# Ffn gate and up: the high and low activation halves in one 512-column product

## The chip, the cores and the metric

The program runs on one core of one Trainium2 chip. Its time is the device time of that core in microseconds. The kernel before took 2307.03 us in the median of three runs (2304.10 to 2308.41). TensorE does the products, ScalarE, VectorE and GpSimd the rest, and SyncE issues nearly all transfers.

## The reference, cut to what matters

Twelve sublayers run one after the other on 256 tokens of width 1024: six mixers (two RWKV, one stick-breaking attention, one sparse attention, two with three kinds of heads) and six feed-forward layers. Only the feed-forward layers are touched. Four of them are of this form, with a SwiGLU of hidden width 2816:

```python
def rms_norm(x, g):
    xf = x.astype(jnp.float32)
    y = xf * lax.rsqrt(jnp.mean(xf * xf, axis=-1, keepdims=True) + RMS_EPS)
    return (y * g.astype(jnp.float32)).astype(x.dtype)

def swiglu(h, w_gu, w_down):
    g, u = jnp.split(h @ w_gu, 2, axis=-1)
    return (jax.nn.silu(g) * u) @ w_down

x = x + swiglu(rms_norm(x, norm_ffn[i]), ffn_w_gu[i], ffn_w_down[i])
```

The other two (layer indices 4 and 5) put a convolution over three neighbouring tokens on the gate, and use GELU:

```python
g, u = jnp.split(h @ w_gu, 2, axis=-1)
g = depthwise_conv_centred(g, cw, cb)
return x + (jax.nn.gelu(g, approximate=False) * u) @ w_dn
```

## The kernel before, in words

Activations lie transposed: 128 channels on the partitions, 256 tokens (S) along the free dimension, eight such tiles (KT) for the width of 1024. Every large product is done in a split form. An operand is cut into a high half, rounded to the type fp32r, and a low half, the rest. Three products of 128x256 are then summed in PSUM: high weight by high activation, high weight by low activation, low weight by high activation (lines 2184 to 2186). A *unit* is one weight block of 1024 by 128 with its 3 x 8 = 24 products; a gate or an up tile of 128 hidden channels is one unit.

SyncE loads the weight blocks into a ring of four (`ring_a`, 512 KB each), and the down blocks into a ring of two (`ring_d`). For each block ScalarE writes the high half (`hi`, line 2269) and VectorE the low half (`lo`, line 2372) into `w_split`, also a ring of four. Semaphores order it all: `w_hi` and `w_lo` count finished halves, `a_used` counts finished units, `dn_hi` and `dn_lo` are the same for the down blocks, and `d_used` counts finished down steps.

A feed-forward layer has 22 tiles of hidden channels, handled in pairs i = 0 to 10 with q = 0 and 1 in a pair. For tile (i, q) TensorE runs `gate_up(i, q)`, two units into the two halves of one bank, B[4+q]. When both are done, VectorE multiplies the bank by the inverse root of the mean square (line 2442), ScalarE applies SiLU (line 2336; GELU on 2339 after the three convolution operations on 2451 to 2456), VectorE multiplies gate by up (2460), ScalarE copies the high half of the result (2342) and VectorE the low half (2464). Only then may `down(i, q)` run: 24 products with the down block into banks 0 to 3, where they are summed over all 22 tiles. TensorE's order is written by hand: `gate_up(i, 0)`, `down(i-1, 1)`, `gate_up(i, 1)`, `down(i, 0)`, so a tile's `down` comes one down step and one gate_up after its own gate_up. The first `down` of a layer has only `gate_up(0, 1)` in front of it. The last two tiles are summed together in `last_two`, after `down(9, 1)`.

Each engine runs its instructions in order. The order on ScalarE and VectorE is that of `tile_pair` in their `ffn`: the splits of two later weight blocks, the split of the down block, then the activation steps of the tile. After the last tile VectorE makes the low halves of the next layer's first blocks, adds banks 0 to 3 to the residual `xT`, and makes the next layer's `h_split`. The inverse root (`root`) is computed on ScalarE once per layer, from sums that TensorE makes (`norm`) behind its first two units.

## Time and profile before

| | |
|---|---|
| median of three runs | 2307.03 us |
| span of the profiled execution, first to last instruction | 2303.6 us |
| granted TensorE clock, mean over the span | 0.988 |
| TensorE busy with products | 2176.2 us (94%) |
| VectorE busy | 1552.0 us (67%) |
| ScalarE busy | 1204.9 us (52%) |
| moved from and to HBM | 141 GB/s over the span |

For the profiled execution only its span is given; the times of the three runs are 0.5 to 4.8 us above it. A matmul's shown duration (283 ns) is longer than its spacing, because matmuls overlap in the pipeline: the pace is read from the starts of successive rows. In the rows, PE is a product, PEld the load of its weights, DVE is VectorE and ACT is ScalarE.

### The profile page before, as it was taken

How to read it: one execution, taken by the hardware profiler on the slowest of the kernel's cores; microseconds unless marked ns; L12 is line 12 of the kernel's file. 1: busy time of each engine (PE TensorE's matmuls, PEld its weight loads, DVE VectorE, ACT ScalarE, POOL GpSimd, SP SyncE). 2: the span in 40 equal slices, each digit the busy share in tenths (PEclk: the TensorE clock that was granted, in tenths of full speed). 3: DMA queues.
4: the chain of work that ended last, by engine and by line, in shares of the span. 5: the costliest groups of instructions: out<-in, count | busy, mean ns of one | idle time of the engine just before them, and what ended most of it. 6: DMA issues, size and time to landing. Idle time of an engine off the chain costs nothing. (4 is left out here: it accounts for less than half of the span.)

```text
span 2303.6 us, 55968 instructions
## 1 busy us (share of the span) xinstructions
PE 2176.2 (94%) x23136; PEld 2079.3 (90%) x23136; DVE 1552.0 (67%) x2405; ACT 1204.9 (52%) x2058; POOL 36.1 (2%) x51
## 2 busy tenths in 40 slices
PE   6887899999999999999989888999999999999998
PEld 6777799999999988899988778999998999898998
DVE  7763465566665688665588735655777777876776
ACT  5733454455544456554458435544676444776443
POOL 0000000000000011000000000000100000100000
PEclk9899999999999999999989999999999999999999
DMA  5310355543455433355533103555333554434553
GB/s 204 128 48 4 110 176 181 180 140 120 153 194 183 163 112 124 123 192 191 183 101 123 54 4 111 192 191 182 129 115 133 193 190 155 147 120 147 182 191 110
DMA packets 88436, 327.16 MB, mean 142 GB/s; under 512 B 9808, under 2 KB 9936, under 8 KB 87632
## 3 DMA queue, kind: packets, MB, share of 16 engines
q1 hardware_dynamic: 87984, 322.66, 41.3%
q8 instruction: 129, 2.11, 0.4%
q0 software_dynamic: 288, 2.10, 0.3%
q14 instruction: 35, 0.29, 0.0%
HBM read 323.67 MB, written 1.05 MB: 141 GB/s over the span
## 5 line engine op out<-in xcount | busy, mean ns | idle before, releaser
L2184 PE MATMUL bank<-h_split,w_split 128*128 128x256 f32 x3176 | 912.7, 287 | 14.3 <-DVE h_split L2403 8.6
L2185 PE MATMUL bank<-h_split,w_split 128*128 128x256 f32 x3176 | 898.1, 283 | 0.0
L2186 PE MATMUL bank<-h_split,w_split 128*128 128x256 f32 x3176 | 897.6, 283 | 0.0
L2372 DVE TENSOR_TENSOR w_split<-ring_a,w_split 128x1024 fp32r<-128x1024 f32 x474 | 568.0, 1224 | 196.9 <-ACT w_split L2269 195.4
L2184 PEld LDWEIGHTS bank<-h_split,w_split 128*128 128x128 f32 x3176 | 602.9, 190 | 26.3 <-DVE h_split L2403 11.3
L2185 PEld LDWEIGHTS bank<-h_split,w_split 128*128 128x128 f32 x3176 | 598.6, 188 | 1.4
L2186 PEld LDWEIGHTS bank<-h_split,w_split 128*128 128x128 f32 x3176 | 597.8, 188 | 0.0
L2269 ACT ACTIVATE w_split<-ring_a 128x1024 fp32r<-128x1024 f32 x474 | 483.4, 1049 | 44.1 <-PE bank L664 23.7
L2206 PE MATMUL bank<-act_split,d_split 128*128 128x256 f32 x1008 | 285.4, 283 | 3.8 <-DVE act_last L2464 2.4
L2207 PE MATMUL bank<-act_split,d_split 128*128 128x256 f32 x1008 | 285.2, 283 | 0.0
L2208 PE MATMUL bank<-act_split,d_split 128*128 128x256 f32 x1008 | 285.1, 283 | 0.0
L2336 ACT ACTIVATE work<-work 128x256 f32<-128x256 f32 x88 | 36.9, 420 | 347.9 <-DVE work L2442 347.9
L2206 PEld LDWEIGHTS bank<-act_split,d_split 128*128 128x128 f32 x1008 | 193.1, 192 | 4.6 <-DVE act_last L2464 2.8
L2208 PEld LDWEIGHTS bank<-act_split,d_split 128*128 128x128 f32 x1008 | 193.2, 192 | 0.0
L2442 DVE TENSOR_TENSOR work<-bank,work 128x512 f32<-128x512 f32 x132 | 90.8, 688 | 151.8 <-PE bank L2186 151.8
L2207 PEld LDWEIGHTS bank<-act_split,d_split 128*128 128x128 f32 x1008 | 192.9, 191 | 0.0
L2439 DVE TENSOR_TENSOR d_split<-ring_d,d_split 128x1024 fp32r<-128x1024 f32 x126 | 153.5, 1218 | 2.5 <-ACT d_split L2333 2.5
L2333 ACT ACTIVATE d_split<-ring_d 128x1024 fp32r<-128x1024 f32 x126 | 131.5, 1043 | 0.0
L2339 ACT ACTIVATE work<-work 128x256 f32<-128x256 f32 x44 | 18.4, 418 | 179.6 <-DVE work L2456 179.6
L2460 DVE TENSOR_TENSOR work<-work 128x256 f32<-128x256 f32 x132 | 56.2, 426 | 64.0 <-ACT work L2336 42.7
L2464 DVE TENSOR_TENSOR act_split<-work,act_split 128x256 fp32r<-128x256 f32 x126 | 53.6, 426 | 61.0 <-ACT act_split L2342 61.0
L2342 ACT ACTIVATE act_split<-work 128x256 fp32r<-128x256 f32 x126 | 52.6, 418 | 61.9 <-DVE work L2460 61.9
(302 smaller groups left out, 3256.4 us busy)
## 6 DMA issues: line engine op xcount, KB each, us to landing
ring_a<-wa SPq DMA_DIRECT2D x474, 512.0 KB, 3.7
ring_d<-wd SPq DMA_DIRECT2D x132, 512.0 KB, 4.3
tab_sb<-tab SPq DMA_DIRECT2D x1, 2384.0 KB, 13.2
hT<-na POOLq DMA_DIRECT2D x2, 1024.0 KB, 5.1
xT<-x SPq DMA_DIRECT2D x1, 1024.0 KB, 4.8
out<-xT SPq DMA_DIRECT2D x1, 1024.0 KB, 3.9
vec_sb<-vec SPq DMA_DIRECT2D x1, 288.0 KB, 4.8
tab_sb<-tab SPq DMA_DIRECT2D x1, 65.0 KB, 4.6
```

The lines of the kernel that those rows point to most:

```text
L2184: mm(dst, w[:, 0, ks], x[:, 0, k, :], start=(k == 0), stop=False)
L2185: mm(dst, w[:, 0, ks], x[:, 1, k, :], start=False, stop=False)
L2186: last = mm(dst, w[:, 1, ks], x[:, 0, k, :], start=False, stop=(k == KT - 1))
L2206: mm(o, w[:, 0, ms], x[:, 0, :], start=(first and m % 2 == 0), stop=False, skip_group_check=True)
L2207: mm(o, w[:, 0, ms], x[:, 1, :], start=False, stop=False, skip_group_check=True)
L2208: return mm(o, w[:, 1, ms], x[:, 0, :], start=False, stop=final, skip_group_check=True)
L2269: A(w_split[:, u % 4, 0, :], ring_a[:, u % 4, :], ACT.Copy).then_inc(s["w_hi"], 1)
L2333: A(d_split[:, q, 0, :], ring_d[:, q, :], ACT.Copy).then_inc(s["dn_hi"], 1)
L2372: v.tensor_tensor(w_split[:, u % 4, 1, :], ring_a[:, u % 4, :], w_split[:, u % 4, 0, :].bitcast(f32), ALU.subtract).then_inc(s["w_lo"], 1)
L2439: v.tensor_tensor(dd[:, 1, :], ring_d[:, q, :], dd[:, 0, :].bitcast(f32), ALU.subtract).then_inc(s["dn_lo"], 1)
L2442: v.tensor_tensor(work[:, 2 * q:2 * q + 2, :], B[4 + q][:, :].rearrange("p (a b) -> p a b", a=2), inv_rms().unsqueeze(1).broadcast_to([P, ...
L2460: v.tensor_tensor(work[:, 2 * q + 1, :], work[:, 2 * q, :], work[:, 2 * q + 1, :], ALU.mult)\
```

## The change

The two products that share the high weight become one. `h_split[:, :, k, :]` holds high and low activation halves, 256 columns each. `wide_unit` multiplies both at once by the high weight, a 128x512 product that fills a whole bank, and then adds the low weight by the high activation into the first 256 columns. A unit has 16 products in place of 24, on the same number of columns: 8 x 512 + 8 x 256 = 24 x 256. Each unit now needs a bank of its own, so tile (i, q) uses banks 4+2q and 5+2q.

The second 256 columns of each bank (the *tail*) have to be added. `gu_half(q, 1)` is the pair of tails of gate and up. ScalarE copies it to `hT` (semaphore `gu_low`), VectorE adds it to the pair of first halves into `work`, waits for its own result, and then multiplies by the inverse root, now from SBUF to SBUF.

The order on ScalarE and VectorE changes too. The splits of the weight blocks for the next pair stand between the activation steps, and the split of the down block stands last in the tile (in the last tile ahead of the last activation step). `last_two` runs the products of the last but one tile for the first four output blocks before it waits for the last tile's activation. SyncE issues a down block ahead of two weight blocks for each tile.

On VectorE, in the first tile of the first feed-forward layer, the program before has these rows (`d_split` is the down block's low half):

```order
L2372 TENSOR_TENSOR w_split<-ring_a,w_split 128x1024 [waits w_hi] x2
L2439 TENSOR_TENSOR d_split<-ring_d,d_split 128x1024 [waits dn_hi,std_ready]
L2442 TENSOR_TENSOR work<-bank,work 128x512 [waits a_used]
L2460 TENSOR_TENSOR work<-work 128x256 [waits silu_ready]
L2464 TENSOR_TENSOR act_split<-work,act_split 128x256 [waits act_hi]
```

And the changed program, at the same place:

```order
L2418 TENSOR_TENSOR w_split<-ring_a,w_split 128x1024 [waits w_hi] x2
L2485 TENSOR_TENSOR work<-bank,hT 128x512 [waits gu_low]
L2489 TENSOR_TENSOR work<-work 128x512 [waits dve_step,std_ready]
L2418 TENSOR_TENSOR w_split<-ring_a,w_split 128x1024 [waits w_hi]
L2508 TENSOR_TENSOR work<-work 128x256 [waits silu_ready]
L2418 TENSOR_TENSOR w_split<-ring_a,w_split 128x1024 [waits w_hi]
L2516 TENSOR_TENSOR act_split<-work,act_split 128x256 [waits act_hi]
L2478 TENSOR_TENSOR d_split<-ring_d,d_split 128x1024 [waits dn_hi]
```

Two weight splits and the down block's split now stand between the product's end and the last row that the first `down` waits for; the down block's split went from the front of the tile to its end.

On VectorE, in the last two tiles of the same layer, before:

```order
L2439 TENSOR_TENSOR d_split<-ring_d,d_split 128x1024 [waits dn_hi]
L2442 TENSOR_TENSOR work<-bank,work 128x512 [waits a_used]
L2460 TENSOR_TENSOR work<-work 128x256 [waits silu_ready]
L2464 TENSOR_TENSOR act_split<-work,act_split 128x256 [waits act_hi]
L2439 TENSOR_TENSOR d_last<-ring_d,d_last 128x1024 [waits dn_hi]
L2442 TENSOR_TENSOR work<-bank,work 128x512 [waits a_used]
L2460 TENSOR_TENSOR work<-work 128x256 [waits silu_ready]
L2464 TENSOR_TENSOR act_last<-work,act_last 128x256 [waits act_hi]
```

And the changed program, at the same place:

```order
L2485 TENSOR_TENSOR work<-bank,hT 128x512 [waits gu_low]
L2489 TENSOR_TENSOR work<-work 128x512 [waits dve_step]
L2508 TENSOR_TENSOR work<-work 128x256 [waits silu_ready]
L2516 TENSOR_TENSOR act_split<-work,act_split 128x256 [waits act_hi]
L2478 TENSOR_TENSOR d_split<-ring_d,d_split 128x1024 [waits dn_hi]
L2485 TENSOR_TENSOR work<-bank,hT 128x512 [waits gu_low]
L2489 TENSOR_TENSOR work<-work 128x512 [waits dve_step]
L2508 TENSOR_TENSOR work<-work 128x256 [waits silu_ready]
L2478 TENSOR_TENSOR d_last<-ring_d,d_last 128x1024 [waits dn_hi]
L2516 TENSOR_TENSOR act_last<-work,act_last 128x256 [waits act_hi]
```

The split of the last down block (`d_last`) stood ahead of the last tile's steps and now stands inside them. The diff:

```diff
-B = [ctx.enter_context(nc.psum_tensor(f"bank{i}", [P, 512], f32)) for i in range(8)]
+banks = ctx.enter_context(nc.psum_tensor("bank", [P, 8, 512], f32))
+B = [banks[:, i, :] for i in range(8)]
+def gu_half(q, a):
+    return banks[:, 4 + 2 * q:6 + 2 * q, a * S:(a + 1) * S]
+def gu_tail(q):
+    return hT[:, 2 * q:2 * q + 2, :]
...
@@ -2120,22 +2129,33 @@
+            def load_down(j, i=0):
+                if L["d"] + j >= 2 or not isinstance(i, int):
+                    sp.wait_ge(s["dn_lo"], i * 2 + (L["d"] + j - 1))
+                sp.dma_start(ring_d[:, j % 2, :], wd[i * 2 + (L["d"] + j), :, :])\
+                    .then_inc(d_loaded[j % 2], 16)
+            def next_tiles(i):
+                for q in range(2):
+                    load_down(2 + q, i)
+                    load(L, 8 + 2 * q, i)
+                    load(L, 9 + 2 * q, i)
...
+            for q in range(2):
+                load_down(q)
+                load(L, 4 + 2 * q)
+                load(L, 5 + 2 * q)
+            with sp.Fori(0, FT // 2 - 2) as i:
+                next_tiles(i)
+            for q in range(2):
+                load_down(FT - 2 + q)
...
@@ -2186,6 +2206,18 @@
+    def wide_unit(L, n, i, bank, x, ready=None):
+        pe.wait_ge(s["w_lo"], i * 4 + (L["us"] + n + 1))
+        w = w_split[:, (L["u"] + n) % 4, :, :]
+        for k in range(KT):
+            if ready:
+                pe.wait_ge(s[ready[0]], ready[1] + k + 1)
+            ks = slice(k * P, (k + 1) * P)
+            mm(bank, w[:, 0, ks], x[:, :, k, :], start=(k == 0), stop=False)
+            last = mm(bank[:, 0:S], w[:, 1, ks], x[:, 0, k, :], start=False, stop=(k == KT - 1))
+        last.then_inc(s["a_used"], 1)
...
@@ -2196,8 +2228,8 @@
-                unit(L, 2 * q + g, i, B[4 + q][:, g * S:(g + 1) * S], h_split,
-                     ready=("h_ready", 8 * L["hs"]) if first and g == 0 else None)
+                wide_unit(L, 2 * q + g, i, B[4 + 2 * q + g], h_split,
+                          ready=("h_ready", 8 * L["hs"]) if first and g == 0 else None)
...
@@ -2217,16 +2249,20 @@
+            pe.wait_ge(s["act_ready"], FT * f + FT - 1)
+            pe.wait_ge(s["dn_lo"], d + FT)
+            for m in range(4):
+                block_of(m, d_split[:, 0, :, :], act_split[:, 0, :, :])
             pe.wait_ge(s["act_ready"], FT * f + FT)
-            pe.wait_ge(s["dn_lo"], d + FT)
-            for m in range(KT):
-                a = block_of(m, d_split[:, 0, :, :], act_split[:, 0, :, :])
-                b = block_of(m, d_last, act_last, final=True)
-                if m == KT - 1:
-                    a.then_inc(s["d_used"], 1)
-                    b.then_inc(s["d_used"], 1)
-                elif m % 2:
-                    b.then_inc(s["down_done"], 1)
+            for b in range(4):
+                for m in (2 * b, 2 * b + 1):
+                    last = block_of(m, d_last, act_last, final=True)
+                last.then_inc(s["down_done" if b < 3 else "d_used"], 1)
+                if b < 2:
+                    for m in (2 * b + 4, 2 * b + 5):
+                        last = block_of(m, d_split[:, 0, :, :], act_split[:, 0, :, :])
+                    if b == 1:
+                        last.then_inc(s["d_used"], 1)
...
@@ -2315,35 +2351,45 @@
+                act.wait_ge(s["a_used"], i * 4 + (u + 2 * q + 2))
+                A(gu_tail(q), gu_half(q, 1), ACT.Copy).then_inc(s["gu_low"], 1)
+                if first and q == 0:
                     root(L)
+                if not final:
+                    hi(L, 2 * q + 4, i)
...
                     A(work[:, 2 * q, :], work[:, 2 * q, :], ACT.Silu).then_inc(s["silu_ready"], 1)
...
+                if not final:
+                    hi(L, 2 * q + 5, i)
+                if final and q:
+                    down_high(q, i, final)
...
                 A(a_[:, 0, :], work[:, 2 * q + 1, :], ACT.Copy).then_inc(s["act_hi"], 1)
+                if not (final and q):
+                    down_high(q, i, final)
...
@@ -2426,21 +2472,21 @@
+                dve.wait_ge(s["gu_low"], i * 2 + (FT * f + q + 1))
+                gu = work[:, 2 * q:2 * q + 2, :]
+                step.did(v.tensor_tensor(gu, gu_half(q, 0), gu_tail(q), ALU.add))
+                if first and q == 0:
                     rms_inverse(L)
-                dd = d_last if final and q else d_split[:, q, :, :]
-                dve.wait_ge(s["a_used"], i * 4 + (u + 2 * q + 2))
-                v.tensor_tensor(work[:, 2 * q:2 * q + 2, :], B[4 + q][:, :].rearrange("p (a b) -> p a b", a=2),
-                                inv_rms().unsqueeze(1).broadcast_to([P, 2, S]), ALU.mult)\
+                step.settle()
+                v.tensor_tensor(gu, gu, inv_rms().unsqueeze(1).broadcast_to([P, 2, S]), ALU.mult)\
                     .then_inc(s["gu_ready"], 1)
...
+                if not final:
+                    lo(L, 2 * q + 4, i)
...
                 v.tensor_tensor(work[:, 2 * q + 1, :], work[:, 2 * q, :], work[:, 2 * q + 1, :], ALU.mult)\
...
+                if not final:
+                    lo(L, 2 * q + 5, i)
+                if final and q:
+                    down_low(q, i, final)
...
                 v.tensor_tensor(a_[:, 1, :], work[:, 2 * q + 1, :], a_[:, 0, :].bitcast(f32), ALU.subtract)\
...
+                if not (final and q):
+                    down_low(q, i, final)
```

## Rows read from the trace of the kernel before

**Rows 1.** The page's busy time: engine, us (share of the span), instructions.

```profile
PE 2176.2 (94%) x23136; PEld 2079.3 (90%) x23136; DVE 1552.0 (67%) x2405; ACT 1204.9 (52%) x2058; POOL 36.1 (2%) x51
```

**Rows 2.** Busy time by stretch, inside a SiLU and a convolution layer: all engines.

```profile
300.00:460.00 160.00, 160.00 (x1337) 160.00 (x1336) 96.41 (x116) 71.20 (x97) 0.00 (x0) 1.00 0.55 188
1790.00:1940.00 150.00, 150.00 (x1254) 150.00 (x1253) 113.41 (x160) 65.31 (x88) 0.00 (x0) 1.00 0.55 186
```

**Rows 3.** Timeline of PE at half the granted clock: start us, us, engine, line.

```profile
1183.18 0.41 PE L2186 MATMUL bank<-h_split,w_split 128*128 128x256 f32 x1
1183.39 0.41 PE L2184 MATMUL bank<-h_split,w_split 128*128 128x256 f32 x1
```

**Rows 4.** Timeline of PE behind a layer's first two units, plain fp32 products.

```profile
295.76 1.02 PE L2175 MATMUL bank<-sq,tab_sb 128*128 128x256 f32 x4
```

**Rows 5.** Groups by line and shape: count, busy us, mean ns, idle before.

```profile
L2442 DVE TENSOR_TENSOR work<-bank,work 128x512 f32<-128x512 f32 x132 | 90.8, 688 | 151.8 <-PE bank L2186 151.8
L2413 DVE TENSOR_TENSOR sq<-sq 128x512 f32<-128x512 f32 x30 | 20.8, 692 | 6.4 <-ACT sq L2309 4.3
L911 ACT ACTIVATE planes<-bank 128x512 f32<-128x512 f32 x44 | 24.5, 594 | 82.8 <-PE bank L546 53.9 <-PE bank L502 27.5 <-PE bank L558 1.3
```

**Rows 6.** Timeline of ACT at the start of the first feed-forward layer.

```profile
295.13 2.00 ACT L2269 ACTIVATE w_split<-ring_a 128x1024 fp32r<-128x1024 f32 x2
297.04 0.45 ACT L2277 ACTIVATE work<-bank,tab_sb 128x256 f32<-128x256 f32 x1
297.53 0.42 ACT L2279 ACTIVATE work<-work 128x256 f32<-128x256 f32 x1
297.85 1.05 ACT L2333 ACTIVATE d_split<-ring_d 128x1024 fp32r<-128x1024 f32 x1
298.92 1.28 ACT L2336 ACT_TABLE_LOAD   x1
```

**Rows 7.** Timeline of DVE there.

```profile
296.22 2.36 DVE L2372 TENSOR_TENSOR w_split<-ring_a,w_split 128x1024 fp32r<-128x1024 f32 x2 [1.13 <-ACT w_split L2269]
299.00 1.23 DVE L2439 TENSOR_TENSOR d_split<-ring_d,d_split 128x1024 fp32r<-128x1024 f32 x1 [0.41 <-ACT d_split L2333]
300.14 0.68 DVE L2442 TENSOR_TENSOR work<-bank,work 128x512 f32<-128x512 f32 x1
```

**Rows 8.** Timeline of PE: the first down product of that layer.

```profile
303.36 0.28 PE L2206 MATMUL bank<-act_split,d_split 128*128 128x256 f32 x1
```

**Rows 9.** Timeline of PE: the first down product of the first convolution layer.

```profile
1781.49 0.39 PE L2206 MATMUL bank<-act_split,d_split 128*128 128x256 f32 x1 [0.67 <-DVE act_split L2464]
```

**Rows 10.** Timeline of DVE in a middle tile of that layer.

```profile
1860.45 0.69 DVE L2442 TENSOR_TENSOR work<-bank,work 128x512 f32<-128x512 f32 x1
1861.41 0.41 DVE L2451 TENSOR_SCALAR work<-work,vec_sb 128x256 f32<-128x256 f32 x1 [0.27 <-DVE work L2442]
1861.97 0.48 DVE L2453 SCALAR_TENSOR_TENSOR work<-work,vec_sb 128x255 f32<-128x255 f32 x1
1862.60 0.48 DVE L2456 SCALAR_TENSOR_TENSOR work<-work,vec_sb 128x255 f32<-128x255 f32 x1
1863.57 0.42 DVE L2460 TENSOR_TENSOR work<-work 128x256 f32<-128x256 f32 x1 [0.48 <-ACT work L2339]
```

**Rows 11.** Timeline of DVE at the end of the first feed-forward layer.

```profile
473.36 0.69 DVE L2442 TENSOR_TENSOR work<-bank,work 128x512 f32<-128x512 f32 x1 [1.50 <-PE bank L2186]
475.44 0.42 DVE L2464 TENSOR_TENSOR act_last<-work,act_last 128x256 fp32r<-128x256 f32 x1 [0.48 <-ACT act_last L2342]
476.39 3.49 DVE L2372 TENSOR_TENSOR w_split<-ring_a,w_split 128x1024 fp32r<-128x1024 f32 x3 [0.52 <-ACT w_split L2269]
```

**Rows 12.** Timeline of PE: the first down product behind the last gate and up products there.

```profile
473.16 0.28 PE L2206 MATMUL bank<-act_split,d_split 128*128 128x256 f32 x1
```

**Rows 13.** Timeline of DVE at the end of the first convolution layer.

```profile
1951.59 0.69 DVE L2442 TENSOR_TENSOR work<-bank,work 128x512 f32<-128x512 f32 x1
1956.11 1.23 DVE L2372 TENSOR_TENSOR w_split<-ring_a,w_split 128x1024 fp32r<-128x1024 f32 x1 [0.52 <-ACT w_split L2269]
```

More of the change, by code:

```diff
@@ L222, in build_program @@
                   "w_hi w_lo dn_hi dn_lo h_raw h_hi act_raw act_hi xm_raw xm_hi  o_hi o_ready "
-                  "gu_ready down_done squared squares_summed first_summed out_done wi_mm wi_ready").split():
+                  "gu_low gu_ready down_done squared squares_summed first_summed out_done wi_mm wi_ready").split():
             sems[n] = ctx.enter_context(nc.semaphore(n))
@@ L2122, in _ @@
                 if L["kind"] == "ffn":
[L2123 to L2138 removed]
+                    def load_down(j, i=0):
[8 more added lines that the diff above has]
+                            load(L, 9 + 2 * q, i)
+                    for j in range(4):
+                        load(L, j)
+                    if L["part"] == 0:
+                        sp.dma_start(tab[:, FIRST_W:TAB_W], tab_in[:, FIRST_W:TAB_W]).then_inc(s["tab_loaded"], 16)
+                    if plan[L["part"] - 1]["kind"] == "rwkv":
+                        sp.wait_ge(s["o_raw"], 5 * plan[L["part"] - 1]["rw"] + 5)
+                    for q in range(2):
[6 more added lines that the diff above has]
+                        load_down(FT - 2 + q)
                 else:
@@ L2316, in ffn, with tile_pair @@
                 f, u = L["d"] // FT, L["u"]
-                def tile_pair(i, final):
+                def tile_pair(i, first, final):
                     for q in range(2):
-                        if not (final and q):
-                            for g in range(2):
-                                n = 2 * q + g + 2
-                                hi(L, n, i)
-                        if isinstance(i, int) and i == 0 and q == 0:
-                            root(L)
-                        act.wait_ge(d_loaded[q], i * 16 + 16 * (L["d"] // 2 + 1))
-                        if final and q:
-                            A(d_last[:, 0, :], ring_d[:, q, :], ACT.Copy).then_inc(s["dn_hi"], 1)
-                        else:
-                            if f or not isinstance(i, int) or i:
-                                act.wait_ge(s["d_used"], i * 2 + (L["d"] + q - 1))
-                            A(d_split[:, q, 0, :], ring_d[:, q, :], ACT.Copy).then_inc(s["dn_hi"], 1)
+                        act.wait_ge(s["a_used"], i * 4 + (u + 2 * q + 2))
+                        A(gu_tail(q), gu_half(q, 1), ACT.Copy).then_inc(s["gu_low"], 1)
+                        if first and q == 0:
+                            root(L)
+                        if not final:
+                            hi(L, 2 * q + 4, i)
                         if L["idx"] < 4:
@@ L2342, in tile_pair, with down_high @@
                         A(a_[:, 0, :], work[:, 2 * q + 1, :], ACT.Copy).then_inc(s["act_hi"], 1)
-                tile_pair(0, False)
+                        if not (final and q):
+                            down_high(q, i, final)
+                def down_high(q, i, final):
+                    act.wait_ge(d_loaded[q], i * 16 + 16 * (L["d"] // 2 + 1))
+                    if final and q:
+                        A(d_last[:, 0, :], ring_d[:, q, :], ACT.Copy).then_inc(s["dn_hi"], 1)
+                    else:
+                        if f or not isinstance(i, int) or i:
+                            act.wait_ge(s["d_used"], i * 2 + (L["d"] + q - 1))
+                        A(d_split[:, q, 0, :], ring_d[:, q, :], ACT.Copy).then_inc(s["dn_hi"], 1)
+                for n in range(early(L), 4):
+                    hi(L, n)
+                tile_pair(0, True, False)
                 with act.Fori(1, FT // 2 - 1) as i:
-                    tile_pair(i, False)
-                tile_pair(FT // 2 - 1, True)
+                    tile_pair(i, False, False)
+                tile_pair(FT // 2 - 1, False, True)
             for L in plan:
@@ L2461, in tile_pair @@
                             .then_inc(s["act_raw"], 1)
+                        if not final:
+                            lo(L, 2 * q + 5, i)
+                        if final and q:
+                            down_low(q, i, final)
                         dve.wait_ge(s["act_hi"], i * 2 + (FT * f + q + 1))
@@ L2465, in tile_pair @@
                             .then_inc(s["act_ready"], 1)
-                tile_pair(0, False)
-                with step.repeat(FT // 2 - 2, 4 if conv else 0, 1) as i:
-                    tile_pair(i, False)
-                tile_pair(FT // 2 - 1, True)
+                        if not (final and q):
+                            down_low(q, i, final)
+                for n in range(early(L), 4):
+                    lo(L, n)
+                tile_pair(0, True, False)
+                with step.repeat(FT // 2 - 2, 6 if conv else 2, 1) as i:
+                    tile_pair(i, False, False)
+                tile_pair(FT // 2 - 1, False, True)
                 for n in range(KT):
```

30 lines of the change are left out of this document (6 added, 24 removed).

## The prediction

> **What bounds the kernel now.** I read the busy times first. TensorE has products under way for 94% of the span, VectorE works for 67% and ScalarE for 52% [rows 1]. By stretch, the feed-forward layers are tighter still: TensorE has no gap in 160 us of a SiLU layer and none in 150 us of a convolution layer, while VectorE is busy 60% and 76% there [rows 2]. So inside these layers only TensorE's pace counts. That pace is 1337 products in 160.00 us, 119.7 ns each, and 119.6 ns in the other layer; both at a granted clock of 1.00. At half the clock the timeline shows 0.21 us from one product of 256 columns to the next [rows 3], which is 256 columns at 1.2 GHz and nothing on top. At 2.4 GHz 256 columns alone would be 106.7 ns. So 13 ns of each 120 at full clock are not columns.
>
> The whole change rests on what these 13 ns are. A slow pace per column (0.47 ns) gives nothing back when columns are merged. A fixed toll per product, or per weight load, is saved 8 times per unit. If a product cannot start sooner than 120 ns after the last one because its weights load meanwhile, then a stream of 213 ns hides the load altogether. The half-clock row is that case: a stream of 213 ns, with its own weight load, with nothing on top. The plain fp32 products behind a layer's first units are a second one: four in 1.02 us, the last shown for 0.38, so 0.213 us between starts at full clock [rows 4, 2].
>
> **The products.** A unit has 24 products now, 24 x 0.1197 = 2.87 us. After, 8 wide ones and 8 narrow ones. The narrow one keeps 0.120. For the wide one the bounds are 0.213 (columns only) and 0.240 (two of today's). I take 0.215, by the rows whose stream is as long. Then a pair costs 0.335 in place of 0.359, and a unit 8 x 0.0245 = 0.196 us less. There are 6 x 44 = 264 units: 51.7 us in all if nothing else comes late. With a toll of 13 ns kept on the wide product (0.2265) it is 0.105 us per unit, 27.7 us in all; with 0.240, nothing.
>
> The Trainium skill ("TensorE: Matmul & The Clock Gate", Back-to-back issue gap) gives N/2.4 + 2.5 ns between matmuls at full clock, so 109 ns at 256 columns and 215.7 at 512. For 256 columns the trace disagrees (119.7). By the rule at both sizes a pair would save 2.6 ns, not 24.5, and the change would give 5.5 us at best before its waits; with 119.7 measured that reading has no chance. By the trace for the narrow and the rule for the wide it is my sum. The same page says that weights are read through a port of their own and take no bandwidth from the running product, which speaks against the toll; no run here shows that yet.
>
> **Steady state.** The new work per tile is one ScalarE copy of 128x512 out of PSUM (0.594 us on a like copy) and one VectorE sum of 128x512 (0.69); the multiply keeps its price, 0.692 from SBUF against 0.688 from PSUM [rows 5]. ScalarE had 71 of 160 us of work and gets 22 tiles x 0.6; it hides it. VectorE in a SiLU layer gets to some 70%, hidden as well. The other half of the question is latency: from the end of gate_up(i, q) the results for down(i, q) must be ready within one down step and one gate_up, 2.87 + 16 x 0.335 = 8.24 us. In a convolution layer the chain inside the loop, by the starts in [rows 10], is: product drained 0.2, copy 0.6, sum 0.69 and its own wait 0.2, multiply to first convolution step 0.96 in the worst row (0.87 where the idle is 0.19), then 0.56, 0.63 and 0.5, a weight split 1.14, gate by up 0.35, second split 1.14, low half 0.35, down split 1.22: 8.4 to 8.5. That misses 8.24 by 0.2; two tiles are in flight, so each tile pays half, 0.1 us, and 20 tiles pay 2 us per layer. A SiLU layer has 1.7 us less in the chain and pays nothing. With the slower wide product the window grows and the loss goes.
>
> **Start of a layer.** Here the first down has only gate_up(0, 1) before it, and the down split has moved to the end of the chain. From the absolute times in the first layer: ScalarE is free of the second split at 297.04 [rows 6]. Then copy 0.51 (0.594 less the 0.1 by which neighbours overlap), root 0.81 to 0.90, a weight split 0.95, table load 1.28, SiLU to 301.2, second weight split to 302.2. VectorE: split done 298.6 [rows 7], sum 299.3, multiply 300.0, weight split 301.2, gate by up 301.65, second split 302.3 to 303.45, low half 303.8, down split 305.0. The first down product started at 303.36 [rows 8]; it will start at 305.05, 1.7 us later. The first four units' gain is swallowed by this, since ScalarE and not TensorE sets 297.04. In the convolution layer the same reckoning gives 1783.0 against 1781.49 [rows 9], 1.5 later.
>
> **End of a layer.** gate_up(10, 1) is done at 473.33: the multiply that waits for it starts at 473.36 [rows 11]. TensorE then has down(9, 1), which began at 473.16 and ends 24 x 0.12 later at 476.04 [rows 12]. The new `last_two` first asks for the last down block's low half, though its first products don't read it. Copy to 473.95, sum 474.7, multiply 475.4, SiLU 475.85, ScalarE's half of `d_last` 1.04 to 476.9, VectorE's half 1.22 to 478.15. TensorE stands from 476.04 to 478.2, 2.1 us. Its twelve early products (1.44 us) then cover the last activation step. VectorE's next row, the splits for the next layer, comes at 478.6 in place of 476.39, so the next layer's start moves by the same 2.1. In the convolution layer the tile before ends its chain 1.7 us after gate_up(10, 1) does, later than the copy at 0.6; with its three extra steps in both tiles the loss is 2.1 + 1.0 = 3.1 (the row that moves is the second of [rows 13]; from the multiply to it were 4.52 us, against 3.03 in [rows 11]).
>
> **Hidden.** SyncE's new order brings a down block and two weight blocks together, once a tile; they are needed a tile later, at an unchanged 1.5 MB per 8.3 us, with DMA at 0.55 of its time [rows 2]. Were the cover gone, a late block would cost part of its landing at every tile, and all gain. The splits stand further ahead of their units than before, so a wait for weights inside a layer is less likely, worth nothing where there was no gap.
>
> **The sum.** 40 of a layer's 44 units count: 40 x 0.196 = 7.84. SiLU layer: 7.84 - 1.7 - 2.1 = 4.0, four of them 16.2. Convolution layer: 7.84 - 2.0 - 1.5 - 3.1 = 1.2, two of them 2.5. Together 18.7 us off the span of 2303.6, so 2284.9; the median of the runs stood 3.4 above that span, so 2288.
>
> **Rivals.** (a) *The toll stays on each product.* 40 x 0.105 = 4.2 us per layer; SiLU layers gain 0.4, convolution layers lose 0.3 (the loop then fits): about 1 us in all, 2306. For it: 120 against 107 needs a cause, and plain fp32 columns, at half the rate, do not show it. Against: at half clock nothing is left of it. (b) *The pace is per column*, the wide product 0.240. Then only the new waits stay: 4 x 3.8 + 2 x 4.6 = 24 us slower, 2331. It decides from 0.227 upwards: there the gain of a pair is 12.7 ns, and 6 x 320 pairs no longer pay for 24 us. For it: no product of this type and 512 columns is in the trace, so 0.47 ns per column is not excluded at full clock; the half-clock row would hide it too. (c) *The waits at both ends are milder* than the hand reckoning, because ScalarE and VectorE run ahead at some step: with half of them gone the gain is 18.7 + 12 = 31, 2276; with all gone 2255. (d) *The change doesn't do what it says*: the wide product is split on the chip into two. That is (b) in time.
>
> **Numbers.** Forecast with 0.215: 48%. (a) 20%, (b) with (d) 16%, (c) 10%, other mishaps (late blocks, a longer chain in the loop) 6%. A difference under 0.2%, 4.6 us, cannot be told from no change here. Faster gets the forecast, (c) and the lower edge of (a): 0.60. Same: most of (a) and the weak edge of the forecast, 0.18. Slower: (b) and the mishaps, 0.22. The forecast's own range is 2279 to 2297. The range over the cases runs from (c)'s 2272 to 2320, which leaves out the outer part of (b) and the far side of (c).
>
> **What would show it.** In the changed profile: wide products in the loop spaced 0.215 to 0.22 and narrow ones 0.12, 56 products a tile where there were 72, and a tile in about 8.25 us where it took 72 x 0.1197 = 8.62. A wait of TensorE for `d_split` at each layer's first down, near 2 us, and one for `d_last` at each layer's end, 2 to 3 us. Short waits at every tile of the two convolution layers, none in the loops of the SiLU layers. A wide spacing over 0.225 makes the forecast wrong through its first term; missing waits at the ends make it wrong through the last ones.

## The result, and the profile after

The changed kernel is slower: 2325.91 us (median of 4 runs, 2323.86 to 2329.68) against 2307.72 us before (4 runs, 2304.1 to 2312.87), a ratio of 1.0078 (95% interval 1.006 to 1.0095, written [1.006, 1.0095] from here on). The forecast was 2288 with a range of 2272 to 2320, so the change went the other way and past the range. The span of its profiled execution is 2323.7 us; of before it was 2303.6.

The page's busy time, and the two new operations of its list of groups (count | busy us, mean ns | idle before):

```profile
PE 2171.3 (93%) x21024; PEld 1972.8 (85%) x21024; DVE 1620.8 (70%) x2537; ACT 1277.6 (55%) x2190; POOL 36.2 (2%) x51
...
L2485 DVE TENSOR_TENSOR work<-bank,hT 128x512 f32<-128x512 f32 x132 | 91.2, 691 | 276.5 <-ACT hT L2357 276.5
L2357 ACT ACTIVATE hT<-bank 128x512 f32<-128x512 f32 x132 | 78.7, 596 | 350.9 <-PE bank L2218 350.6
```

2112 products are gone and TensorE is busy 5 us less than in [rows 1], where the forecast's 0.196 us for each of 264 units would have it 52 less. Part of the gap is the clock, since this profile has more time at half clock. Copy and sum cost what was expected of them (0.596 and 0.691). So the first reading is the products. Timeline of TensorE inside a tile:

```profile
319.69 0.40 PE L2217 MATMUL bank<-h_split,w_split 128*128 128x512 f32 x1
319.92 0.28 PE L2218 MATMUL bank<-h_split,w_split 128*128 128x256 f32 x1
320.04 0.39 PE L2217 MATMUL bank<-h_split,w_split 128*128 128x512 f32 x1
320.27 0.28 PE L2218 MATMUL bank<-h_split,w_split 128*128 128x256 f32 x1
320.38 0.39 PE L2217 MATMUL bank<-h_split,w_split 128*128 128x512 f32 x1
```

Read the starts: 0.23 from a wide product to the narrow one, 0.12 or 0.11 back. Over the pairs at full clock the medians are 233 and 118 ns, and the median of the pairs is 350 (the mean is 352, since about one pair in a tile takes 388). Three products of 256 columns took 359.1 by the forecast's 119.7; by the starts it is 359.9. So a pair saves between 7 and 9 ns and not 24.5; 8.6, from a pair of 350.5, is used below, and whole layers give 8.3 (see the first experiment).

TensorE's new waits (us in total, times, longest), against 2.4 for `act_last` and 1.3 for `act_split` before:

```profile
PE bank L2238 <- DVE d_last L2478: 16.7, 6, 4.3
PE bank L2238 <- DVE d_split L2478: 11.2, 7, 2.4
```

The start of the first layer: VectorE, then TensorE's first down product (answers to [rows 7, 8]):

```profile
298.61 0.69 DVE L2485 TENSOR_TENSOR work<-bank,hT 128x512 f32<-128x512 f32 x1
...
302.21 1.23 DVE L2418 TENSOR_TENSOR w_split<-ring_a,w_split 128x1024 fp32r<-128x1024 f32 x1 [0.52 <-ACT w_split L2305]
303.35 0.42 DVE L2516 TENSOR_TENSOR act_split<-work,act_split 128x256 fp32r<-128x256 f32 x1
303.68 1.22 DVE L2478 TENSOR_TENSOR d_split<-ring_d,d_split 128x1024 fp32r<-128x1024 f32 x1
```
```profile
305.05 0.35 PE L2238 MATMUL bank<-act_split,d_split 128*128 128x256 f32 x1 [1.57 <-DVE d_split L2478]
```

It starts at 305.05, the forecast's figure, against 303.36 before. In a second profile of each kernel it is 303.67 against 301.86. The end of the layer (answers to [rows 11, 12]):

```profile
474.96 0.42 DVE L2508 TENSOR_TENSOR work<-work 128x256 f32<-128x256 f32 x1 [0.48 <-ACT work L2364]
475.91 1.23 DVE L2478 TENSOR_TENSOR d_last<-ring_d,d_last 128x1024 fp32r<-128x1024 f32 x1 [0.52 <-ACT d_last L2381]
477.06 0.42 DVE L2516 TENSOR_TENSOR act_last<-work,act_last 128x256 fp32r<-128x256 f32 x1
477.39 3.49 DVE L2418 TENSOR_TENSOR w_split<-ring_a,w_split 128x1024 fp32r<-128x1024 f32 x3
```
```profile
477.29 0.36 PE L2238 MATMUL bank<-act_split,d_split 128*128 128x256 f32 x1 [2.02 <-DVE d_last L2478]
```

TensorE waits 2.02 us until the low half of the last down block is split. The splits for the next layer start at 477.39 where they started at 476.39. In the first convolution layer the two waits are 2.37 and 4.30 us, and something comes behind them. Timeline of TensorE at its first down step (answers to [rows 9]), and the window of the stretch (busy us of PE, PEld, DVE, ACT, POOL, then the granted clock):

```profile
1793.06 0.50 PE L2238 MATMUL bank<-act_split,d_split 128*128 128x256 f32 x1 [2.37 <-DVE d_split L2478]
1793.36 0.42 PE L2239 MATMUL bank<-act_split,d_split 128*128 128x256 f32 x1
1793.58 0.42 PE L2240 MATMUL bank<-act_split,d_split 128*128 128x256 f32 x1
...
1796.56 0.28 PE L2239 MATMUL bank<-act_split,d_split 128*128 128x256 f32 x1
1796.67 0.28 PE L2240 MATMUL bank<-act_split,d_split 128*128 128x256 f32 x1
...
1797.51 0.39 PE L2217 MATMUL bank<-h_split,w_split 128*128 128x512 f32 x1
```
```profile
1793.30:1796.70 3.40, 3.40 (x18) 3.40 (x18) 3.26 (x6) 0.93 (x2) 0.00 (x0) 0.52 0.74 251
```

The products stand 0.21 apart for 3.4 us: the granted clock has fallen to the lower of its two levels, 1.2 GHz. The step takes 4.45 us in place of 24 x 0.12 = 2.88, so 1.6 us are lost on top of the wait of 2.37. The same is seen from 1970.6 on, at the end of the wait of 4.30:

```profile
1970.82 0.55 PE L2238 MATMUL bank<-act_split,d_split 128*128 128x256 f32 x1 [4.30 <-DVE d_last L2478]
```

It doesn't follow each time. The second convolution layer has the same wait at its start, and the granted clock stays at 1.00 behind it (2135.9 to 2139.3):

```profile
PE bank L2238 <- DVE d_last L2478: 4.3, 1, 4.3
PE bank L2238 <- DVE d_split L2478: 2.4, 1, 2.4
```

Inside the first convolution layer a down step starts late at every second turn, by 0.08 us (0.20 against 0.12 from the product ahead of it), and once by 0.36. In the second convolution layer only one step is late, by 0.14; why the two differ is open. The rows are of the first:

```profile
1863.30 0.28 PE L2218 MATMUL bank<-h_split,w_split 128*128 128x256 f32 x1
1863.50 0.36 PE L2238 MATMUL bank<-act_split,d_split 128*128 128x256 f32 x1
...
1871.96 0.28 PE L2218 MATMUL bank<-h_split,w_split 128*128 128x256 f32 x1
1872.08 0.28 PE L2238 MATMUL bank<-act_split,d_split 128*128 128x256 f32 x1
```

### The profile page after: what moved, and what is told of

Its sections match the earlier page's. It is cut to its first block and busy times, and to the rows that moved or that the text cites. A ratio compares the mean times of both kernels' runs of the same rounds, so it can differ in the third digit from the quotient of the medians.

```text
span 2323.7 us, 52097 instructions
## 1 busy us (share of the span) xinstructions
PE 2171.3 (93%) x21024; PEld 1972.8 (85%) x21024; DVE 1620.8 (70%) x2537; ACT 1277.6 (55%) x2190; POOL 36.2 (2%) x51
## 5 line engine op out<-in xcount | busy, mean ns | idle before, releaser
L2217 PE MATMUL bank<-h_split,w_split 128*128 128x512 f32 x2112 | 752.9, 397 | 10.5 <-DVE h_split L2449 5.8
L2418 DVE TENSOR_TENSOR w_split<-ring_a,w_split 128x1024 fp32r<-128x1024 f32 x474 | 578.2, 1224 | 127.8 <-ACT w_split L2305 126.4
L2218 PE MATMUL bank<-h_split,w_split 128*128 128x256 f32 x2112 | 592.3, 280 | 0.0
L2305 ACT ACTIVATE w_split<-ring_a 128x1024 fp32r<-128x1024 f32 x474 | 494.9, 1049 | 42.7 <-PE bank L673 23.5
L2217 PEld LDWEIGHTS bank<-h_split,w_split 128*128 128x128 f32 x2112 | 397.0, 188 | 108.4 <-DVE h_split L2449 8.2
L2218 PEld LDWEIGHTS bank<-h_split,w_split 128*128 128x128 f32 x2112 | 397.3, 188 | 0.0
L2204 PE MATMUL bank<-h_split,w_split 128*128 128x256 f32 x1064 | 317.0, 298 | 2.9 <-DVE h_split L2449 1.5
L2238 PE MATMUL bank<-act_split,d_split 128*128 128x256 f32 x1008 | 289.4, 287 | 27.9 <-DVE d_last L2478 16.7
L2206 PE MATMUL bank<-h_split,w_split 128*128 128x256 f32 x1064 | 301.7, 284 | 0.0
L2205 PE MATMUL bank<-h_split,w_split 128*128 128x256 f32 x1064 | 300.8, 283 | 0.0
L2485 DVE TENSOR_TENSOR work<-bank,hT 128x512 f32<-128x512 f32 x132 | 91.2, 691 | 276.5 <-ACT hT L2357 276.5
L2357 ACT ACTIVATE hT<-bank 128x512 f32<-128x512 f32 x132 | 78.7, 596 | 350.9 <-PE bank L2218 350.6
L2204 PEld LDWEIGHTS bank<-h_split,w_split 128*128 128x128 f32 x1064 | 202.1, 190 | 8.9 <-DVE h_split L2449 2.5
L2205 PEld LDWEIGHTS bank<-h_split,w_split 128*128 128x128 f32 x1064 | 202.9, 191 | 1.4
L2206 PEld LDWEIGHTS bank<-h_split,w_split 128*128 128x128 f32 x1064 | 201.2, 189 | 0.0
```

Of the source, the lines that this page charges most:

```text
L2204: mm(dst, w[:, 0, ks], x[:, 0, k, :], start=(k == 0), stop=False)
L2205: mm(dst, w[:, 0, ks], x[:, 1, k, :], start=False, stop=False)
L2206: last = mm(dst, w[:, 1, ks], x[:, 0, k, :], start=False, stop=(k == KT - 1))
L2217: mm(bank, w[:, 0, ks], x[:, :, k, :], start=(k == 0), stop=False)
L2218: last = mm(bank[:, 0:S], w[:, 1, ks], x[:, 0, k, :], start=False, stop=(k == KT - 1))
L2238: mm(o, w[:, 0, ms], x[:, 0, :], start=(first and m % 2 == 0), stop=False, skip_group_check=True)
```

## The experiments

Each ratio is against runs of the kernel before on the same chip. Behind each expectation stands what came of it.

**Only the wide product undone.** The theory after the result: the wide product gains about a third of the forecast, and the longer chain at both ends of a layer costs what it was said to. The rival: the wide product gains nothing.

```diff
-mm(bank, w[:, 0, ks], x[:, :, k, :], ...)
+mm(bank[:, 0:S], w[:, 0, ks], x[:, 0, k, :], ...)
+mm(bank[:, S:2 * S], w[:, 0, ks], x[:, 1, k, :], ...)
```

> The changed kernel with each wide product cut back into two of 256 columns, one into each half of the same bank; banks, copy of the tails, sum and all orders stay as changed. Theory A (the wide product does pay, but only the 8.6 ns per pair that the changed trace shows: 233 + 117.5 ns against 3 x 119.7): 40 x 8 x 8.6 ns = 2.75 us more per layer, less the 0.2 us waits in the loops of the convolution layers, which then fit: 2325.9 + 14 = 2340 us. Rival B (the pace is per column and nothing is saved by merging): 2326 us, the same. Rival C (the wide products are slower, for instance because they write a whole bank): under 2322 us.

2337.77 us, 1.0132 [1.0111, 1.0153], near theory A's 2340. The wide product is worth 12 us (2337.77 - 2325.91), with some 6 us of uncertainty from four runs on each side; it gains, but little. The layers say it more sharply: from its first down product to its last, a SiLU layer free of half-clock stretches takes 180.6 us here and 177.9 in the changed kernel. That is 2.67 us for 320 pairs, 8.3 ns each.

**Only the new order.** Products and epilogue of before (no copy, no sum), everything else of the change.

> The changed kernel with the products and the epilogue of before: three products of 256 columns, both units in one bank, no copy of tails, no sum, the multiply straight from the bank. The new order of the splits, of the loads and of the last two tiles stays. Theory A (a good part of the loss is the order: the down block's split stands at the end of the chain): a wait of TensorE for d_split at each layer's start of about 1 us and for d_last at each end of 0.8 us (2 us in convolution layers), together 10 to 12 us over before: 2318 us. Rival B (the order is free, and the two new operations in the chain alone make the waits): 2308 us. If A and B share it, the time tells how.

2315.12 us, 1.0035 [1.0023, 1.0046], between A and B and nearer to A. The order alone costs 8 us. TensorE waits 6.9 us for `d_last` and 6.6 for `d_split`. The ladder is then: order +8, copy and sum +22 (1.0035 to 1.0132), wide product -12. The copy and the sum, hidden by the busy shares, are the dearest part. At both ends of a layer they lie in the chain that TensorE waits for: the two waits are 13.5 us together here and 26.4 with copy and sum. That is 12.9 of the 22 us. The profile of the first experiment also has 71.7 us at half clock where the one of this has 54.9, and how much of that is chance isn't known.

**The chain mended.** The down block's split stands at the front of the last tile, and ahead of the activation in the first, and the wait for `d_last` stands behind the early products.

```diff
+if final and q:
+    down_low(q, i, final)
...
-pe.wait_ge(s["dn_lo"], d + FT)
+pe.wait_ge(s["dn_lo"], d + FT - 1)
 for m in range(4): block_of(m, d_split[:, 0, :, :], act_split[:, 0, :, :])
+pe.wait_ge(s["dn_lo"], d + FT)
```

> The changed kernel with the down block's split moved out of the chain in the first tile (ahead of the two weight splits) and in the last tile (ahead of its activation steps), and with last_two waiting for the last down block only when it reads it. Wide products, copy and sum stay. Theory A (the waits at both ends, and the half-clock stretches behind them, are where the gain went): the waits at the start vanish in the four SiLU layers and fall to about 1 us in the two others, those at the end vanish in SiLU layers and fall to 1 to 2 us in the others: 20 us less, 2306 us, and to 2298 us if the additional half-clock stretches (79 us of half clock in the changed profile against 55) go with them. Rival B (the waits only stand in for something later in the chain, such as the adds of the next layer's start): 2320 us or more.

2309.27 us, 1.0015 [1.0002, 1.0027], 3 us over theory A's first figure. Some 15 us of the loss (1.0078 to 1.0015) go with an edit that touches no product. The waits for `d_last` are gone; what is left at the ends is (us in total, times, longest):

```profile
PE bank L2238 <- DVE act_last L2526: 6.1, 2, 3.1
PE bank L2238 <- DVE d_split L2485: 2.3, 2, 1.2
PE bank L2238 <- DVE act_split L2526: 1.0, 2, 0.5
```

In its profile (2305.49 us, the fastest of the ten runs) 58 us are at half clock where the changed kernel had 82, and one stretch still stands at the end of a wait of 3.1 us. The small gain of the wide product brings the kernel back to the time of before, no further.

**The products by themselves.** TensorE alone on data in SBUF, one shape after the other; nothing of the reference is computed.

> None of the reference is computed. TensorE alone runs streams of independent products at full clock, 24 to 64 of each kind, every one with its own weights: fp32r of 256, 512 contiguous, 512 as two runs of 256, 384 and 128 columns; 256 and 512 columns with weights 64 columns wide; bf16 of 256 and 512; plain fp32 of 256. Then fp32r 256 and 512 once more while VectorE and ScalarE stream fp32 through SBUF. Theory A (a pace per column of 0.455 ns for fp32r, nothing or 1 to 3 ns per product): 512 gives 233, 384 gives 175, 256 gives 117 to 120; bf16 gives 109 and 216; narrow weights change nothing. Rival B (the load of weights slows the stream beside it, a toll of some 10 to 20 ns per load that grows with the stream): 64-column weights bring 256 columns to about 112 and 512 to about 222. Rival C (the two runs cost): contiguous 512 is at 216, two runs at 233. Rival D (the other engines' traffic costs): alone 109 and 216, beside them 120 and 233.

One row for each shape; the interval of the starts over the count less one is the spacing. From the top: 256, 512 and 512 columns in two runs of 256 in fp32r, 256 and 512 in bf16, 256 in plain fp32, and 512 fp32r beside busy VectorE and ScalarE:

```profile
L80 PE MATMUL bank<-xr,wr x64: 283/283/283, 19.9 to 27.4; 128*128 128x256 f32 x64
L83 PE MATMUL bank<-xr,wr x48: 389/389/398, 27.5 to 38.2; 128*128 128x512 f32 x48
L87 PE MATMUL bank<-xr,wr x48: 389/389/389, 38.5 to 49.1; 128*128 128x512 f32 x48
L102 PE MATMUL bank<-xb,wb x64: 272/272/283, 83.1 to 90.0; 128*128 128x256 bf16 x64
L105 PE MATMUL bank<-xb,wb x47: 379/379/379, 90.3 to 100.2; 128*128 128x512 bf16 x47
L108 PE MATMUL bank<-x_sb,w_sb x48: 379/379/379, 100.4 to 110.6; 128*128 128x256 f32 x48
L114 PE MATMUL bank<-xr,wr x48: 388/389/397, 118.5 to 129.1; 128*128 128x512 f32 x48
```

From the unrounded starts, in ns: fp32r 120.0, 227.3, 226.7; bf16 109.3 and 215.8; plain fp32 215.9; beside traffic 227.3. Less the columns at 2.4 GHz, fp32r keeps 13.3 at 256 and 14.0 at 512 (384 columns: 173.9, 13.9 over). So a product of this type has a toll of about 13.5 ns that does not shrink from 256 to 512 columns. None of the theories gave just this: the pace per column (A) would be 233 at 512, the traffic (D) and the two runs (C) cost nothing, and weights of 64 columns took 113.6 ns at 256, near B's 112, but 229.8 at 512, where B said 222. What makes the toll was not found. At half clock there is none: 0.21 us in [rows 3] and behind the wait at 1793 above. The forecast's second witness for 0.215, plain fp32, is another type and has only 2.6 ns.

**Wide and narrow in turn.** In the kernel the wide one measured 233 to 235, not 227. Is it the turn, the summing into one bank, or traffic?

> None of the reference is computed. TensorE alone again: wide (two runs of 256) and narrow fp32r products in turn without sums, sums over 32 wide products in one bank, sums over 48 narrow ones in one bank, four units as in the changed kernel (8 x wide and narrow into one bank), weights of 32 and 96 columns with 256 and 512 moving columns, 256 columns with the same weights each time, and units again while VectorE and ScalarE stream. In e4_bench alone-standing wide products came every 227 ns and narrow ones every 120; in the changed kernel it is 233 and 117.5, a pair 350.5 against 347. Theory A (the toll is that of a weight load beside a stream and goes with its columns): 32 columns of weights near 110 ns at 256 and 217 to 220 at 512, 96 columns between 64 and 128 (117, 228). Rival B (the toll is fixed per fp32r product): 120 and 227 for every weight width. For the pair: if summing into a bank in place costs, the sums show it (over 227 and 120) and the products in turn don't; if taking turns costs, both do; if neither, it is the traffic of the other engines.

Wide and narrow in turn, each product closed; then wide alone and narrow alone, each summed in one bank:

```profile
L88 PE MATMUL bank<-xr,wr x32: 395/398/404, 19.2 to 30.2; 128*128 128x512 f32 x32
L91 PE MATMUL bank<-xr,wr x32: 277/281/285, 19.5 to 30.4; 128*128 128x256 f32 x32
L94 PE MATMUL bank<-xr,wr x32: 388/389/398, 30.6 to 37.6; 128*128 128x512 f32 x32
L97 PE MATMUL bank<-xr,wr x48: 278/283/284, 37.8 to 43.5; 128*128 128x256 f32 x48
```

A pair in turn takes 353.4 ns (236.5 + 116.9), summed as in a unit 353.4, beside busy VectorE and ScalarE 353.2. Alone they would make 227.0 + 119.8 = 346.8. Taking turns costs 6.6 ns per pair, and neither sums nor traffic have a part in it. Why is open. Of the theories on the toll neither holds, since it isn't simply a matter of the weights' width, nor is it the same for every width: 256 columns took 113.3, 113.6, 116.0 and 120.0 with 32, 64, 96 and 128 weight columns, while 512 columns took 231.2, 229.8, 230.1 and 227.3. New weights aren't what is paid for either: with the same weights loaded for each of the 256-column products it is 119.5.

**A version of parts.** In the first and the last tile of a layer the chain is what counts, in between the products. So: the mended kernel, with the narrow products and epilogue of before in the first tile and the last.

```diff
+if first or (isinstance(i, int) and i == FT // 2 - 1 and q):
+    unit(L, 2 * q + g, i, B[4 + 2 * q][:, g * S:(g + 1) * S], h_split, ready=ready)
+else:
+    wide_unit(L, 2 * q + g, i, B[4 + 2 * q + g], h_split, ready=ready)
```

> The kernel of e3_mend, but the first and the last tile of each layer with the products and the epilogue of before (three narrow products, no copy, no sum); the 20 tiles between keep the wide products. Theory A (a pair in the loop saves 8.6 ns, and all the rest of the loss stands in the chains of the first and the last tile): 38 units x 8 x 8.6 ns = 2.6 us per SiLU layer with nothing lost at the ends; in the convolution layers 2.6 less some 1.6 of small waits in the loop; together 12 to 14 us less than before: 2294 us. Rival B (the next layer's start hangs on VectorE, and the later splits of the loop and the early products of last_two push it back whatever the last tile does): 2302 to 2306 us.

2302.24 us (8 runs), 0.9966 [0.9952, 0.998]: 0.3% faster than before and faster than the changed kernel, but 8 us short of theory A and in rival B's range. A SiLU layer takes 175.8 us from its first down product to its last, against 178.3 before and 177.9 in the changed kernel: the 2.5 us of theory A (2.6) are there. They are there in the mended kernel too (175.9). (The first product that reads `act_last` can't be compared between them, since nine more products stand ahead of it in the new `last_two`.) Theory A failed in the convolution layers, which take 181.4 and 181.5 us against 179.9 before, and in the mixer, which takes 286.9 us in this profile against 282.0 (more on it below). TensorE waits 1.2 us for `d_split` at the second down step and 2.2 for `act_last`, and 3.4 us at half clock stand behind the latter in both layers.

**One more place in the chain.** The same, with the second weight split of the loop behind the down block's split.

> e5_hybrid with the second weight split of each loop tile behind the down block's split on ScalarE and VectorE, so that the chain up to the down step is about 0.7 us shorter. Theory A (in the convolution layers the chain is longer than the window by 0.2 us, which showed as a wait of 0.08 us at every second step): these waits go, 1.6 us less than e5_hybrid, 2292 us. Rival B (VectorE has no slack in a convolution tile, and the waits move to w_split or grow): 2296 us or more.

2303.3 us, 0.997 [0.9959, 0.9982]: no difference to the last one, as rival B had it in time. But the run doesn't test theory A, whose premise was gone: the late steps of 0.08 us are in the traces of the changed and the mended kernel and not in the one of the version of parts, where between the second down step and the last tile none starts late. There was nothing left for this order to save.

**The RWKV mixer.** One difference was left. From the third feed-forward layer's end to the fourth's first down product, before and the order alone took 282.0 us, and the five profiled kernels that copy tails to `hT` took 286.1 to 287.9, with the same instructions. Is it `hT`, which the mixer uses, or chance? The changed kernel was profiled once more, the kernel before too, and the version of parts was run with its tails in `sq`:

> The changed kernel once more, unedited. Its first profile has 79 us at half clock in 14 stretches, the profile before 55 us in 8. Theory A (the new waits of 2 to 4 us at the layers' ends bring the additional stretches): stretches stand again behind the layer starts and ends (near 1793 and 1970 us), the total is again near 79 us. Rival B (they fall by chance of the execution, many of them in the RWKV mixers, whose instructions are the same in both kernels): the places change and the total is between 50 and 80 us.

> The mended and partly narrow kernel (the hybrid, 2302.2, span 2300.9), with one edit: the 128x512 copy of the tails goes to another part of the memory (blocks 4 to 7 of sq) instead of hT, which the RWKV mixer uses too. Open is why the stretch from the second feed-forward layer after it to the next (the second RWKV mixer, whose instructions are the same in all kernels) took 282.0 us in the profiles of before and of the order alone, and 286 to 289 in every profile of a kernel that copies tails to hT. Theory A, the place hT matters (something in the mixer reads or waits for it): the stretch takes 282 to 283 here and the time falls to 2297 to 2299. Theory B, the phase of the clock's drops (half-clock stretches of 3.4 us each fall between 1289 and 1417 us in those profiles, none in before) and not the memory: the stretch stays at 286 to 289 and the time at 2301 to 2304.

```diff
-return hT[:, 2 * q:2 * q + 2, :]
+return sq[:, 4 + 2 * q:6 + 2 * q, :]
```

> The kernel before, unedited, profiled once more. If the stretch between the third and the fourth feed-forward layer is set by the kernel's instructions, it takes 282.0 us again with no half-clock stretch between 1186 and 1407 us from the span's start. If it is chance from one execution to the next, it can come out at 285 to 289 here, with such stretches, and then the 5 us are no part of what the change does. Expected span 2303 to 2305 in the first case, 2307 to 2310 in the second.

The changed kernel: 289.4 us there. Its half clock sums to 69 us, where its first profile has 82 (79 without the stretch at the program's end). The stretches at 1793 and 1970 us stand again, as theory A had it, and most of the others moved, as B had it. Tails in `sq`: 2300.52 us, 0.9973 [0.9962, 0.9984], 284.2 there. That lies between the two theories, but 0.9973 shows no gain over 0.9966. The kernel before, once more: 286.6, with half clock for 17 us in between. So chance from one execution to the next is enough for the difference. It isn't excluded that `hT` adds a little, since all six profiles with tails in `hT` have 286 us or more and the four without have 282.0, 282.0, 284.2 and 286.6. The window of that mixer, first of before, then of before once more (granted clock behind the busy times):

```profile
1200.00:1407.00 207.00, 177.84 (x4307) 158.70 (x4306) 133.80 (x208) 112.09 (x204) 0.00 (x0) 1.00 0.19 63
```
```profile
1200.00:1407.00 207.00, 181.13 (x4285) 161.59 (x4284) 129.71 (x198) 107.78 (x193) 0.00 (x0) 0.96 0.18 61
```

Same instructions, clock 1.00 once and 0.96 once. The forecast's profile was lucky in this mixer and an ordinary one as a whole. Its span was 2303.6; the spans of 12 runs of the kernel before on the last chip go from 2298.9 to 2307.2 with a median of 2303.7, and the second profile, 2307.2, is at their upper end.

## Why the prediction was wrong

**The wide product: failed, and it decides the sign.** The step that failed is "then a stream of 213 ns hides the load altogether", which set the price of the wide product at 0.215. The toll stays with every product, as rival (a) said: 227 alone, and 233 to 235 in turn with a narrow one. The pair gives 8.6 ns for 24.5. Over 6 x 320 pairs that is 16.5 us for 47.0: 30.5 of the 39 us between the forecast's span and the measured one. The forecast's own decision point was 0.227; the kernel is on the wrong side of it. Both witnesses hid the toll: at half clock 256 columns show none, and plain fp32 has almost none. Neither was this type at full clock, and the prediction inferred a cause (the load hides behind a long stream) from two durations that were alike.

**The start of a layer: right in mechanism, somewhat too dear.** In the first layer the shift is 1.7 us as forecast, 1.8 between the second profiles. That 305.05 agrees to the last digit is luck, since the same kernel had 303.67 the second time. Counted from the last product of the layer ahead, the first down product came 1.3 us later in the second layer and 1.0 to 1.1 in the third, the fifth and the sixth, where 1.5 to 1.7 were reckoned. Six starts cost some 7 us for 9.8.

**The end of a layer: right.** The waits for `d_last` are 2.0 us in a SiLU layer and 4.3 in a convolution layer, 16.7 in all. Of the 4.3 the kernel before already had 1.2 as a wait for `act_last`, so the loss is 2.0 and 3.1 a layer, 14.3 in all, where 2.1 and 3.1 gave 14.6.

**The loop of a convolution layer: right in kind, too dear.** In the first convolution layer 0.08 us at every second tile where 0.1 at each was reckoned, in the second one late step: 1.2 us for 4.0. The longer pair widened the window, as the prediction said it would. The SiLU loops have no wait.

**Hidden work: right** for ScalarE, VectorE (70% of the span) and the transfers: no wait for a late block joined the list.

**Missing from the sum: what follows a wait.** Between a layer's first and last down product neither profile of the kernel before has time at half clock. The first profile of the changed kernel has five stretches of 3.4 us there and the second four, each at or behind one of the new waits. What one costs shows where only it differs: the second SiLU layer took 179.4 us with a stretch, the first 177.9 without. Over the ten profiles of the whole kernel, TensorE's waits at down products compare like this:

| wait | of them with a half-clock stretch at or behind it |
|---|---|
| 4.1 to 4.3 us | 6 of 6 |
| 2.0 to 3.1 us | 13 of 28 |
| under 1.9 us | none |

So a long wait of this kind should be priced with a part of 1.5 us on top. The 20.1 us between the spans then add up so: pairs -16.5, ends 14.3, late down steps 1.2, five stretches 7.4, starts 7, the mixer 3.9 (which chance alone can make, by the second profile of before). That is 17.3. The rest is 0.3 to 0.6 us in each layer; part of it is that whole layers show 8.3 ns a pair and not 8.6, the remainder is open.

**The rivals.** (a) was right in mechanism (the toll), but 2306 was too low, since the pair in turn costs more than its 0.2265 and 0.12, and since its waits had no half clock behind them. (b) came nearest in time (2331) by luck: its pace per column gives 240 ns, and the wide product measured 227 alone. The misjudgement was to give (a) only 20%: 120 against 107 at full clock was the only row of this very type and clock, and it showed the toll. Its 0.105 us a unit is also a little high: by its own prices it is 0.100 to 0.103. (c) didn't come about, since the waits at both ends stood nearly in full. (d) is out: 2112 products are gone, and the wide one takes less than two narrow ones (233 against 240).

## What to carry to other kernels

Price a merged instruction by rows of the same type at the same clock. Where none exists, hold the toll for fixed and ask whether the change survives that. Work that the busy shares hide is still paid where a layer starts or ends. Put only what the next product reads into that chain, and use the long form (copy, sum, wide product) only in the middle, where the engines run ahead. Check in the trace that a wait is still there before you edit it away. Before explaining a difference of 0.2% between two profiles, profile the unchanged kernel a second time.

## What the runs showed of the hardware

- An fp32r product costs its columns at 2.4 GHz and some 13.5 ns more: 110.8, 120.0, 173.9 and 227.3 ns for 128, 256, 384 and 512 columns (at 128 columns it is 57 ns over, so something else sets the pace there). The Trainium skill ("TensorE: Matmul & The Clock Gate", Back-to-back issue gap) gives N/2.4 + 2.5 ns: bf16 agrees at both sizes (109.3, 215.8), and plain fp32 too if its 256 columns count as 512 (215.9); fp32r does not.
- Wide and narrow fp32r products in turn cost 353 ns a pair in the bare stream, apart 347.
- The granted clock falls to half for 3.4 us or longer (up to 20.5) at places that in part differ between executions of one kernel: 8 stretches in one profile of the kernel before, 9 in the other, with a difference of 4.6 us in one mixer. All six waits of TensorE of 4.1 to 4.3 us at a down product had such a stretch at or behind them, and none of those under 1.9 us.
